# Other beats for the first layers' steps, SSD heads in pairs over both halves of TensorE's columns, and the decay's cap taken for several heads at once

## What is computed

```python
xdt = ch(xh * dt[..., None])
da_cs = jnp.cumsum(ch(dt * a), axis=2)
decay = jnp.exp(jnp.where(causal, da_t[..., :, None] - da_t[..., None, :], -jnp.inf))
cb = jnp.einsum('bclgn,bcsgn->bcgls', cm, bm)
y_diag = jnp.einsum('bcgls,bcgels,bcsgep->bclgep', cb, decay, xdt)
```

## Time and profile before

| | |
|---|---|
| median of 3 runs | 3545.67 us (3544.63 to 3546.02) |
| profiled execution | 3542.9 us |
| its span | 3541.1 us (1.8 us lie outside it) |
| PE busy | 3474.8 us (98%) |
| DVE, ACT, POOL busy | 2738.2 (77%), 1887.5 (53%), 1701.3 us (48%) |
| mean granted clock of TensorE | 0.996 |

### The profile page before, as it was taken

The page is one execution under the profiler, slowest core; times in us unless marked ns, Lnnn a source line. Parts: engine busy times, 40 slices in busy tenths (PEclk is TensorE's granted clock), DMA queues, the critical chain, the costliest instruction groups (busy, mean ns, idle before and its releaser), DMA issues.

```text
span 3541.1 us, 53042 instructions
## 1 busy us (share of the span) xinstructions
PE 3474.8 (98%) x19584; PEld 2992.7 (85%) x19584; DVE 2738.2 (77%) x4083; ACT 1887.5 (53%) x2857; POOL 1701.3 (48%) x1473
## 2 busy tenths in 40 slices
PE   8999999999999999999999999999999999999999
PEld 7887788888877788887888888888888888888888
DVE  8768887679989976687888758877688888658875
ACT  6555785455555554675544434444665544444443
POOL 4324672267778742144466406653143666306640
PEclk9999999999999999999999999999999999999999
DMA  5544456555555556644555665556544555665566
GB/s 191 168 155 143 160 181 186 187 187 171 180 165 169 174 161 189 194 143 129 187 186 189 183 189 188 186 183 190 188 138 143 189 185 187 186 187 189 186 184 179
DMA packets 177042, 624.39 MB, mean 176 GB/s; under 512 B 19784, under 2 KB 25616, under 8 KB 175760
## 3 DMA queue, kind: packets, MB, share of 16 engines
q1 hardware_dynamic: 171216, 606.11, 54.5%
q10 hardware_dynamic: 5568, 14.89, 1.1%
HBM read 618.75 MB, written 2.17 MB: 175 GB/s over the span
## 4 chain that ended last, share of the span: by engine, by line
PE 72%; DVE 10%; POOL 5%; issue 2%; ACT 2%; ACTq 0%; POOLq 0%; DVEq 0%
PE psG L533 43%; PE psG L531 23%; DVE WL L1275 3%; PE psG L530 3%; POOL SQ L1742 1%; ACT WH L770 1%; POOL SQ L1761 1%; DVE sdx L1288 1%; POOL sdx L1744 1%; POOL GV L1883 1%; DVE Et L1545 1%; DVE Et L1552 1%; PE psM L556 0%; DVE Y L1280 0%; PE psM L514 0%
## 5 line engine op out<-in xcount | busy, mean ns | idle before, releaser
L533 PE MATMUL psG<-H,WH 128*128 128x512 f32 x5655 | 2022.4, 398 | 0.0
L1275 DVE TENSOR_TENSOR WL<-RAW,WH 128x1024 fp32r<-128x1024 f32 (+1 forms) x1162 | 1495.9, 1287 | 518.1 <-ACT WH L770 516.7
L770 ACT ACTIVATE WH<-RAW 128x1024 fp32r<-128x1024 f32 (+1 forms) x1162 | 1214.1, 1045 | 869.2 <-PE psG L533 849.2
L531 PE MATMUL psG<-H,WL 128*128 128x256 f32 x6032 | 1663.5, 286 | 0.2
L533 PEld LDWEIGHTS psG<-H,WH 128*128 128x128 f32 x5655 | 1066.9, 189 | 234.0
L531 PEld LDWEIGHTS psG<-H,WL 128*128 128x128 f32 x6032 | 1143.9, 190 | 44.5 <-issue 9.6
L533 PE MATMUL psG<-Y,WH 128*128 128x512 f32 x2792 | 988.8, 397 | 0.0
L531 PE MATMUL psG<-Y,WL 128*128 128x256 f32 x2944 | 802.1, 281 | 1.0 <-DVE Y L1280 1.0
L533 PEld LDWEIGHTS psG<-Y,WH 128*128 128x128 f32 x2792 | 524.6, 188 | 119.2
L531 PEld LDWEIGHTS psG<-Y,WL 128*128 128x128 f32 x2944 | 555.6, 189 | 15.9 <-issue 1.4
L1892 POOL TENSOR_SCALAR fou<-fsu,PAR 128x256 f32<-128x256 f32 x88 | 177.9, 2022 | 564.6 <-DVE fsu L1317 564.6
(11 more groups left out here) (352 smaller groups left out, 3616.0 us busy)
## 6 DMA issues: line engine op xcount, KB each, us to landing
RAW<-in_w_up SPq DMA_DIRECT2D x352, 512.0 KB, 3.6
RAW<-in_w_o_in SPq DMA_DIRECT2D x162, 512.0 KB, 3.7
RAW<-in_w_e_in SPq DMA_DIRECT2D x128, 512.0 KB, 3.6
RAW<-in_w_down SPq DMA_DIRECT2D x128, 512.0 KB, 3.5
RAW<-in_w_in SPq DMA_DIRECT2D x112, 512.0 KB, 3.6
RAW<-in_w_o SPq DMA_DIRECT2D x72, 512.0 KB, 3.6
RAW<-in_w_e_out SPq DMA_DIRECT2D x64, 512.0 KB, 4.6
RAW<-in_w_o_out SPq DMA_DIRECT2D x64, 512.0 KB, 4.3
```

Of the source, the lines that this page charges most:

```text
L531: ins = e.matmul(o[:, 0:T], wl, x[:, 0:T], start=False, stop=False, skip_group_check=True)
L533: ins = e.matmul(o, wh, x, start=False, stop=last)
L770: copy = lambda o, i, scale=1.0: e.activation(o, i, ACT.Copy, scale=scale)
L1275: tt(WL_[c % NRAW][:, 0:n], RAW_[c % NRAW][:, 0:n], WH_[c % NW][:, 0:n].bitcast(F32), SUB).then_inc(sem("wl"), 1)
```

## The change

**Beats.** The heads of the first layer start 2 beats later behind the gates, the gates' second transpose 2 beats later, the LRU's steps from its product on 2 beats later. The SSD layer's C.B products move 2 beats, its sums of squares 1 beat and their sum over partitions 2 beats later. `z` gets a tenth buffer. **Squares.** POOL squares each part of an mLSTM head as soon as it is there, in four steps (beats 12 to 15 of the head) instead of one. **SSD heads.** TensorE multiplies two heads in one place, by turns in both halves of the columns. DVE caps the targets' sums at the source's own for a group's eight heads in one instruction, and for four heads' second half in another; ACT's exponential, now two instructions per head, adds the negated own sum as its bias; dt goes into `Xk`, which DVE now writes out of PSUM instead of ACT; DVE's product with C.B is one instruction per head and stands one beat later. Two start-up loads share a semaphore, and some steps wait on other counts. The core of the diff:

```diff
--- before.py
+++ after.py
@@ schedule @@
     S.event("gates", 0, S.end_of("k", 7) + 3)
     for h in range(4):
-        S.event("head", h, S.events[("gates", 0)] + 9 + 16 * h)
+        S.event("head", h, S.events[("gates", 0)] + 11 + 16 * h)
     for g in range(8):
         x3 = S.end_of("sx", g * 4 + 3)
-        S.event("cb", g, S.end_of("sC", g) + 14)
+        S.event("cb", g, S.end_of("sC", g) + 16)
...
-        S.event("gsum", g, x3 + (48 if g < 7 else 34))
-        S.event("gnorm", g, x3 + (55 if g < 7 else 35))
+        S.event("gsum", g, x3 + (49 if g < 7 else 34))
+        S.event("gnorm", g, x3 + (57 if g < 7 else 35))
@@ pe, lstm @@
-            for _ in at("gates", b - 7):
+            for _ in at("gates", b - 9):
                 use = take("ct")
                 w.wait_ge(sem("gate_rows"), 1)
...
             for h in at("head", b - 21):
-                w.wait_ge(sem("h_ssq"), h + 1)
+                w.wait_ge(sem("h_ssq"), 4 * h + 4)
                 colsum(("hc", h), hacc)
-            for n in at("lru", b - 10):
+            for n in at("lru", b - 12):
@@ pe, ssd @@
             for hd in at("shead", b - 5):
                 g, k = divmod(hd, 8)
                 if k % 2 == 0:
-                    use = take(("py", hd // 2))
-                use = small[("py", hd // 2)]
+                    continue
+
+                use = take(("py", hd // 2))
                 w.wait_ge(small[("xk", g, 1)].sem, small[("xk", g, 1)].out)
                 w.wait_ge(sem("s_w"), hd + 1)
-                r = slice(64 * (k % 2), 64 * (k % 2) + 64)
-                e.matmul(use.ap[r, 0:T], Xk[g % 2][:, k * 64:k * 64 + 64], Et[hd % 3][:, 0:T], start=True, stop=False)
-                ready(use, e.matmul(use.ap[r, P:T], Xk[g % 2][:, 512 + k * 64:512 + k * 64 + 64], Et[hd % 3][:, T:T + P],
-                                    start=False, stop=True))
-                py_done[hd] = use.done
+                for q, (to, part) in enumerate(((slice(0, T), slice(0, T)), (slice(P, T), slice(T, T + P)))):
+                    for side in range(2):
+                        r = slice(64 * side, 64 * side + 64)
+                        col = q * 512 + (k - 1 + side) * 64
+                        ins = e.matmul(use.ap[r, to], Xk[g % 2][:, col:col + 64], Et[(hd - 1 + side) % 3][:, part],
+                                       start=q == 0, stop=q == 1)
+                ready(use, ins)
+                py_done[hd - 1] = py_done[hd] = use.done
@@ act_prog @@
                 if n >= 9:
-                    w.wait_ge(sem("h_y"), n - 8)
+
+                    w.wait_ge(sem("gate_rows"), 1)
+                if n >= 10:
+                    w.wait_ge(sem("h_y"), n - 9)
                 half("z", n)
...
-            for n in at("lru", b - 11):
+            for n in at("lru", b - 13):
...
                 copy(ncs, use.ap[:, 0:128], -1.0)
+                copy(pcs, use.ap[:, 0:128])
                 copy(dtk, use.ap[:, 128:256], 0.5).then_inc(use.sem, 1)
...
-            for g in at("xk", b - 1):
-                for hf in range(2):
-                    use = small[("xk", g, hf)]
-                    w.wait_ge(sem("small"), use.done)
-                    if g >= 2:
-                        w.wait_ge(sem("small"), py_done[(g - 2) * 8 + 7])
-                    copy(Xk[g % 2][:, hf * 512:(hf + 1) * 512], use.ap).then_inc(use.sem, 1)
             for hd in at("shead", b - 1):
-                w.wait_ge(sem("s_min"), hd + 1)
-                e.activation(Et[hd % 3], Et[hd % 3], ACT.Exp).then_inc(sem("s_exp"), 1)
+                g, k = divmod(hd, 8)
+                E = Et[hd % 3]
+                w.wait_ge(sem("s_min0"), g + 1)
+                w.wait_ge(sem("s_min1"), 2 * g + k // 4 + 1)
+                w.wait_ge(sem("small"), py_done[hd - 3]) if hd > 2 else None
+                e.activation(E[:, 0:T], csb[:, k * T:(k + 1) * T], ACT.Exp, bias=ncs[:, hd:hd + 1])
+                e.activation(E[:, T:T + P], csd[:, k % 4 * P:(k % 4 + 1) * P], ACT.Exp,
+                             bias=ncs[:, 64 + hd:65 + hd]).then_inc(sem("s_exp"), 1)
@@ dve, ssd @@
+            for g in at("xk", b - 1):
+                for hf in range(2):
+
+                    use = small[("xk", g, hf)]
+                    w.wait_ge(sem("small"), use.done)
...
+                    w.wait_ge(small["dt"].sem, small["dt"].out)
+                    tt(Xk[g % 2][:, hf * 512:(hf + 1) * 512].rearrange("p (h c) -> p h c", h=8),
+                       use.ap.rearrange("p (h c) -> p h c", h=8),
+                       dtk[:, hf * 64 + g * 8:hf * 64 + g * 8 + 8].unsqueeze(2).broadcast_to([P, 8, 64]), MUL).then_inc(use.sem, 1)
+            c = csb.rearrange("p (h t) -> p h t", h=8)
             for hd in at("shead", b):
                 g, k = divmod(hd, 8)
-                E = Et[hd % 3]
-                w.wait_ge(sem("csb"), 16 * (g + 1))
-                w.wait_ge(small["dt"].sem, small["dt"].out)
-                w.wait_ge(sem("small"), py_done[hd - 3]) if hd > 2 else None
-                ts(E[:, 0:T], csb[:, k * T:(k + 1) * T], ncs[:, hd:hd + 1], 0.0, ADD, MIN)
-                ts(E[:, T:T + P], csb[:, k * T + P:(k + 1) * T], ncs[:, 64 + hd:65 + hd], 0.0, ADD, MIN).then_inc(sem("s_min"), 1)
-            for hd in at("shead", b - 2):
+
+                if k == 0:
+                    w.wait_ge(sem("csb"), 16 * (g + 1))
+                    w.wait_ge(small["dt"].sem, small["dt"].out)
+                    tt(c[:, :, 0:P], c[:, :, 0:P],
+                       pcs[:, g * 8:g * 8 + 8].unsqueeze(2).broadcast_to([P, 8, P]), MIN).then_inc(sem("s_min0"), 1)
+                if k % 4 == 0:
+                    w.wait_ge(sem("s_exp"), hd) if hd else None
+                    tt(csd.rearrange("p (h t) -> p h t", h=4), c[:, k:k + 4, P:T],
+                       pcs[:, 64 + hd:64 + hd + 4].unsqueeze(2).broadcast_to([P, 4, P]), MIN).then_inc(sem("s_min1"), 1)
+            for hd in at("shead", b - 3):
                 g, k = divmod(hd, 8)
                 E, cb = Et[hd % 3], CBt[g % 2]
                 w.wait_ge(sem("s_exp"), hd + 1)
                 w.wait_ge(small[("cb", g)].sem, small[("cb", g)].out)
-                stt(E[:, 0:T], E[:, 0:T], dtk[:, hd:hd + 1], cb[:, 0:T], MUL, MUL)
-                stt(E[:, T:T + P], E[:, T:T + P], dtk[:, 64 + hd:65 + hd], cb[:, T:T + P], MUL, MUL).then_inc(sem("s_w"), 1)
+                tt(E, E, cb, MUL).then_inc(sem("s_w"), 1)
@@ pool, lstm @@
-            for h in at("head", b - 15):
-                w.wait_ge(small[("pn", h, 3)].sem, small[("pn", h, 3)].out)
-                w.wait_ge(sem("small"), small[("hc", h - 1)].done) if h else None
-                squares(hacc, hs, "h_ssq")
+            for i in range(4):
+                for h in at("head", b - 12 - i):
+
+                    w.wait_ge(small[("pn", h, i)].sem, small[("pn", h, i)].out)
+                    if i == 0:
+                        w.wait_ge(sem("small"), small[("hc", h - 1)].done) if h else None
+                        step(tt(hacc, hs[0], hs[0], MUL), "h_ssq")
+                    else:
+                        sq_free()
+                        own.up(tt(sq, hs[i], hs[i], MUL))
+                        w.wait_ge(own.sem, own.n)
+                        w.wait_ge(sem("h_ssq"), 4 * h + i)
+                        step(tt(hacc, hacc, sq, ADD), "h_ssq")
```

More of the change, by code:

```diff
@@ L379, in build @@
     ncs, dtk = slots("ncs", 2, 16, 128)
+    pcs = slots("pcs", 1, 44, 128)[0]
+    csd = slots("csd", 1, 40, 4 * P)[0]
     sd_s = slots("sds", 3, 17)
@@ L386, in build @@
     sacc, sr = slots("sq_", 2, 38)
-    gsq = slots("gsq", 3, 42)
+    gsq = slots("gsq", 2, 42) + sd_t[:1]
     dts, dtv, dto, dtz = slots("dt", 4, 28)
@@ L572, in lstm @@
                 gates_add(16 + y, v_s[y % 3])
-                w.wait_ge(sem("idn"), 16)
+                w.wait_ge(sem("con"), 32)
                 use = take(("vt", y))
@@ L956, in gates @@
                 e.activation(gz[0:4, :], gz[0:4, :], ACT.Ln, bias=KC[0:4, 3:4]).then_inc(sem("gate_soft"), 1)
-            for _ in at("gates", b - 5):
+            for _ in at("gates", b - 8):
                 w.wait_ge(sem("gate_rows"), 1)
@@ L960, in gates @@
                 e.dma_start(scr_m[1], gG[0:4, :]).then_inc(sem("st_m1"), 16)
-            for _ in at("gates", b - 8):
+            for _ in at("gates", b - 10):
                 use = small["ct"]
@@ L1019, in lru @@
                 e.activation(i, use.ap[:, T:2 * T], ACT.Tanh, bias=halves[:, 16 + n:17 + n], scale=0.5).then_inc(use.sem, 1)
-            for n in at("lru", b - 13):
+            for n in at("lru", b - 15):
                 r, i, l2 = lr[n % 2], li[n % 2], ll2[n % 2]
@@ L1028, in lru @@
                 e.activation(r, r, ACT.Ln, bias=one_c).then_inc(sem("l_ln"), 1)
-            for n in at("lru", b - 16):
+            for n in at("lru", b - 18):
                 w.wait_ge(sem("l_dif"), n + 1)
                 e.activation(lr[n % 2], lr[n % 2], ACT.Exp, scale=0.5).then_inc(sem("l_exp"), 1)
```

(20 more changed lines are left out.)

28 lines of the change are left out of this document (14 added, 14 removed).

## The result

The changed kernel takes 3504.51 us (median of 4 runs, 3501.08 to 3505.91), the kernel before 3545.15 us beside it (4 runs). The ratio is 0.9889, 95% interval 0.9875 to 0.9902: 40.6 us or 1.1% less. The forecast was 3491 us, 54 less. The direction and the range held; a quarter of the gain is missing. The profiled execution took 3501.08 us, its span 3499.3 us, clock 0.998.

What follows compares the result with a forecast made beforehand. TensorE was taken to set the pace, busy 66.36 of 68.00 us per middle SSD group. From 3542.9 us, 21.8 (first layer) and 32.5 (SSD) gave 3488.6; the median runs 2.8 higher, so 3491, range 3477 to 3517.

Steps and rivals of the forecast that it cites:

- first layer: First layer's shifted beats, squares in parts and clock recovery: 21.8 us won; the rival that it gives nothing had 0.12.
- pairs on TensorE: SSD heads multiplied in pairs, column halves overlapping: 0.70 us won per pair, 22.4 us over 32 pairs.
- wait on the decay product: TensorE's SSD wait on VectorE's decay product: 6.1 us falls to 2.0, so 4.1 us won.
- sums of squares: SSD layer: asked for 2 beats later, started 1 later, so GpSimd's wait goes: 4.1 us won.
- SSD, VectorE: SSD decay steps fall from 16.39 to 7.3 us per group, VectorE to about 53; 4.1 us of waits won.
- I leave 0.25 us per group, 2.0 in all: Wait left on the SSD decay product, located at a group's last head, behind the split and x step.
- a new line on `Et` with 32 entries: Sign that would show the forecast wrong: TensorE waiting on the SSD decay product 32 times.
- The lower bound of -10: Worst case for the decay product's wait in the SSD layer: each group's four pairs late by 0.5 us.
- pairs waiting for VectorE: Rival, SSD: odd head's product late for every pair; decides at 1.6 us per pair, 90 us at 2.8; chance 0.04.
- full overlap, but each half in order: SSD pairs, upper bound and figure taken: 0.88 us chain, 1.14 with the change of width, 22.4 us won.
- No overlap: Rival, SSD pairs: column halves run one after another, 1.58 us per pair, 14.1 us less gain, 3505; chance 0.21.
- each change of half costing: Rival, SSD pairs: alternating halves pays 0.26 us four times, 2.36 us per pair, 16.6 us lost, 3530; chance 0.06.
- What the shifts push back is covered: First layer: LRU's last tile has enough beats of cover after the shifts; otherwise 2.8 us lost once.

Runs made afterwards that it cites:

- experiment 7: Changed kernel with the first layer's beats (gates, heads, LRU) and its squares in one go as in the kernel before: 3520.97 us.
- experiment 1: Changed kernel with a pair's products head after head in the same place instead of by turns: 3503.77 us.
- experiment 3: Changed kernel with VectorE's product of decay and C.B one beat earlier: 3500.11 us.
- Experiments 3 to 6: Changed kernel with decay product a beat earlier, 3500.11 us; pair a beat later, 3499.34; that plus sum two beats later, 3491.56; all three, 3483.92.
- experiments 3 and 4: Changed kernel with VectorE's decay product a beat earlier, 3500.11 us; or with the pair and its following steps a beat later in seven groups, 3499.34 us.
- experiment 8: Kernel before with only the pairs' products added, by turns at the odd head's place; decay steps and beats as before: 3536.64 us.
- experiment 2: Changed kernel with heads multiplied singly at their own places as in the kernel before, all else changed: 3548.46 us.

## Why the prediction was right, and where it was off

| term | forecast | measured |
|---|---|---|
| first layer | 21.8 | 17.0 (starts of jobs; 0.6 of it are start-up), 16.5 (experiment 7) |
| pairs on TensorE | 22.4 | 31.7 |
| wait on the decay product | +4.1 | -14.7 |
| sums of squares | 4.1 | 4.1 |
| C.B | 1.9 | 1.9 |
| sum | 54.3 | 40.0, of 40.6 |

The start of the same job, in the SSD layer ahead of its heads, before (L530) and after (L532):

```profile
712.19 0.40 PE L530 MATMUL psG<-H,WH 128*128 128x512 f32 x1
695.22 0.40 PE L532 MATMUL psG<-H,WH 128*128 128x512 f32 x1
```

It starts 17.0 us earlier; a job ahead of the first changed step already starts 0.6 us earlier (215.96 and 215.40). In experiment 1's kernel that early job starts 1.0 us later than in the changed one, so the start-up varies by this much. The clock of the SSD layer stands in no row of the table; the dip at 1180 us costs 0.17 x 7.78 = 1.3 us.

**The failed step** is "SSD, VectorE": "I leave 0.25 us per group, 2.0 in all". It is 20.8 us. Two things in it were wrong. VectorE was to fall to 53 us of a group; it fell to 59.55. The new steps took 11.4 us in place of 7.3, since the estimate by columns came from one row of 1.21 us, and the twenty splits took 3.0 us more than before. And the place was looked for only at the group's last head, behind splits and x step. The trace has the longest wait at the third pair, where VectorE has worked for 25 us without a gap, the last part of it with a convolution and four splits of 1.47 to 1.76 us, two of them right in front of the product. With one split less there (experiment 3) 8.0 us stay. ScalarE, with its second exponential per head, was no bound, as forecast. The sign that was named for this, a new line on `Et` with 32 entries, came with 21. The lower bound of -10 was too near as well. The rival that names this, pairs waiting for VectorE, has the right mechanism; it costs 20.8 / 32 = 0.65 us per pair, not the 1.6 from which it decides. Part of the error is hidden in the sum by luck: 9.3 us too little for the pairs stands against 18.8 too much for this wait. Experiments 3 to 6 show that the loss was a matter of places: one beat here, one there and two at the sum, and 20.6 us come back.

**Pairs.** Direction right, size 9.3 us too small. The bound "full overlap, but each half in order" counted 0.88 us along a chain that ties each half's record to the other's; the halves aren't tied (experiment 1). The change of width, 0.26 us, was rightly counted once per pair. No overlap and each change of half costing are refuted: a pair adds 6.57 - 5.56 = 1.01 us to its job (894.00, 900.57 and 906.13), where they say 1.58 and 2.36. The forecast's own figure is 1.14. The Trainium skill, "TensorE: Matmul & The Clock Gate", section "The mechanism", lets a weight load overlap with running products only in another row group and has products start strictly in the queue's order. Across two column halves that share all rows neither holds here: 0.80 us for eight records with eight sets of weights, and in experiment 1 an odd head's first record starts at 871.96 while the even head's second instruction, ahead of it in the code, starts at 872.41 at the earliest (the halves told apart by the distances; the profile doesn't name them).

**First layer.** The waits fell about as said: gates 3.3 to 0.5, squares 12.1 to 3.3 (2.6 forecast), and the clock stayed at 1.00 with waits up to 1.7 us. Missing are the LRU's product, which waits 1.6 us and not 0, and the WL wait of 3.2 us with its dip, 0.07 x 6.78 + 0.11 x 10 = 1.6 us. These are 6.4 us and the squares 0.7; the gap is 4.8, so 2.3 us came from somewhere that isn't assigned. "What the shifts push back is covered" looked at LRU's last tile and not at VectorE's queue in between.

**Sums of squares and C.B** came as forecast. With 12 to 13 us less of waits on the product in front (experiments 3 and 4), the first no longer holds: the cover was the other stall.

## What to carry over

When one operand of a product gets less slack, go through the queue of the engine that makes it at every place where it is needed, not only at the one that looks tightest: here VectorE's queue was 1.6 us behind at the third pair, and the forecast looked at the fourth. And before another engine is called late, its instruction must be given to the right head: the exponential that stood next to the late product was the next pair's, and the right one had been done for 4.8 us. A stall that goes uncovers the next one, so a step's place should be moved together with those of its followers; the pair's, the sum's and the product's move gave 4 to 5, 8 and 8 us in turn, while the pair's and the product's, each alone, gave about a third of the wait that they removed. Removing instructions from an engine buys less than its busy time says if other instructions take longer beside the new forms, as here: compare the mean of an unchanged instruction before and after.

## What was not expected of the hardware

Two products of 64 columns in different halves of the array run fully side by side: 0.80 us for both by turns, 0.81 one after the other, 0.80 for one.

A large job of 16 blocks without small work takes 5.55 to 5.57 us in most such SSD jobs of the kernels with pairs that were looked at (19 of 27 in the changed one, with 7 of 5.63 or 5.64), also with the old decay steps (experiment 8), and 5.64 or 5.65 in all 7 of the kernel before (967.87 to 973.51) and in all 6 of experiment 2, which has single heads. What sets the pace wasn't settled; it is 0.08 of the 0.99 us that a pair saves.

VectorE's split WL took between 1.21 and 1.77 us, with a mean of 1251 ns before and 1402 after in the same work.
